# Second attention of a two-block layer: scores as three one-pass products, GpSimd beside the rotation of the queries

## What is computed

```python
def mla(c_q_raw, c_kv_raw, k_rope_raw, positions, q_norm, kv_norm, w_uq, w_ukv):
    q = (rmsnorm(c_q_raw, q_norm) @ w_uq).reshape(B, S, H, NOPE_DIM + ROPE_DIM)
    kv = (rmsnorm(c_kv_raw, kv_norm) @ w_ukv).reshape(B, S, H, NOPE_DIM + V_DIM)
    k_nope, v = kv[..., :NOPE_DIM], kv[..., NOPE_DIM:]
    cos, sin = rope_tables(positions, q.dtype)
    q_rope = apply_rope(q[..., NOPE_DIM:], cos[:, :, None, :], sin[:, :, None, :])
    k_rope = apply_rope(k_rope_raw, cos, sin)
    q_full = jnp.concatenate([q[..., :NOPE_DIM], q_rope], axis=-1)
    k_full = jnp.concatenate([k_nope, jnp.broadcast_to(k_rope[:, :, None, :], (B, S, H, ROPE_DIM))], axis=-1)
    return causal_block_attention(q_full, k_full, v)
...
def one_block(args):                       # in causal_block_attention
    s = jnp.einsum('bqhd,bkhd->bhqk', q_blk, k).astype(jnp.float32) * scale
    s = jnp.where(k_idx[None, :] <= q_idx[:, None], s, jnp.finfo(jnp.float32).min)
    pr = jax.nn.softmax(s, axis=-1)
    return jnp.einsum('bhqk,bkhd->bqhd', pr.astype(v.dtype), v)
```

## Time and profile before

| what | value |
|---|---|
| median of 3 runs | 899.24 us (898.68 to 899.51) |
| profiled execution | 898.62 us |
| its span | 896.9 us, mean granted clock of TensorE 0.999 of 2.4 GHz |
| busy: PE, DVE, ACT, POOL | 889.4, 398.5, 343.4, 497.5 us |
| first attention's steps | about 146 to 206 us |
| second attention's steps | about 387 to 450 us |

### The profile page before, as it was taken

One profiled execution on the slowest core, in us unless ns is written; L12 is line 12 of the kernel. 1 busy time (PEld: TensorE's weight loads), 2 busy tenths in 40 slices (PEclk: granted clock), 3 DMA queues, 4 the chain that ended last, 5 costly groups with the idle time before them and its releaser, 6 DMA issues.

```text
span 896.9 us, 12872 instructions
## 1 busy us (share of the span) xinstructions
PE 889.4 (99%) x4488; PEld 732.2 (82%) x4488; DVE 398.5 (44%) x690; ACT 343.4 (38%) x693; POOL 497.5 (55%) x515
## 2 busy tenths in 40 slices
PE   9999999999999999999999999999999999999998
PEld 7889887777779888876779888888888888888887
DVE  2753485677742743866667511111111112223672
ACT  4333403567715130566648532222222223233421
POOL 7988785321475877923336554444444445555453
PEclk9999999999999999999999999999999999999999
DMA  6342363212222422321013332233222323233213
GB/s 219 118 140 85 104 169 98 66 48 94 72 74 72 137 94 82 107 71 48 25 48 94 117 119 94 94 99 102 102 94 94 117 94 94 94 97 105 72 56 117
DMA packets 29467, 85.77 MB, mean 96 GB/s; under 512 B 5192, under 2 KB 8160, under 8 KB 29424
## 3 DMA queue, kind: packets, MB, share of 16 engines
q1 hardware_dynamic: 24528, 78.65, 26.7%
q10 hardware_dynamic: 4896, 6.53, 2.6%
HBM read 80.93 MB, written 2.10 MB: 93 GB/s over the span
## 4 chain that ended last, share of the span: by engine, by line
PE 96%; DVE 1%; ACT 1%; issue 1%; POOL 1%; ACTq 0%; POOLq 0%; DVEq 0%
PE bank L505 28%; PE bank L507 28%; PE bank L506 28%; PE bank L562 5%; PE bank L750 2%; PE bank L1085 2%; PE bank L849 1%; POOL w_lo L458 1%; PE bank L841 1%; PE bank L878 1%; ACT h L1486 0%; DVE negmax L2032 0%; PE bank L729 0%; DVE h L2039 0%; ACT PT L1330 0%
## 5 line engine op out<-in xcount | busy, mean ns | idle before, releaser
L458 POOL TENSOR_TENSOR w_lo<-raw,w_hi 128x256 fp32r<-128x256 f32 (+1 forms) x420 | 409.6, 1004 | 205.7 <-ACT w_hi L1330 199.8
L505 PE MATMUL bank<-aT_hi,w_hi 128*128 128x512 f32 (+1 forms) x584 | 225.8, 387 | 0.0
L507 PE MATMUL bank<-aT_hi,w_lo 128*128 128x512 f32 (+1 forms) x584 | 222.4, 381 | 0.0
L506 PE MATMUL bank<-aT_lo,w_hi 128*128 128x512 f32 (+1 forms) x584 | 222.2, 380 | 0.0
L505 PE MATMUL bank<-w_hi,aT_hi 128*128 128x512 f32 (+3 forms) x576 | 218.3, 379 | 0.5 <-POOL w_lo L458 0.4
L507 PE MATMUL bank<-w_hi,aT_lo 128*128 128x512 f32 (+3 forms) x576 | 213.0, 370 | 0.0
L506 PE MATMUL bank<-w_lo,aT_hi 128*128 128x512 f32 (+3 forms) x576 | 212.9, 370 | 0.0
L450 POOL TENSOR_SCALAR w_hi<-raw 128x1024 fp32r<-128x1024 f32 x70 | 77.3, 1105 | 173.7 <-PE bank L507 142.9
L1330 ACT ACTIVATE w_hi<-raw 128x1024 fp32r<-128x1024 f32 x70 | 74.1, 1060 | 231.4 <-PE bank L507 218.5
L507 PEld LDWEIGHTS bank<-aT_hi,w_lo 128*128 128x128 f32 x584 | 109.8, 188 | 20.9
L505 PEld LDWEIGHTS bank<-aT_hi,w_hi 128*128 128x128 f32 x584 | 110.2, 189 | 19.9 <-issue 0.2
(11 more groups left out here) (228 smaller groups left out, 887.6 us busy)
## 6 DMA issues: line engine op xcount, KB each, us to landing
raw<-in_weights SPq DMA_DIRECT2D x141, 512.0 KB, 3.3
x<-in_x ACTq DMA_DIRECT2D x4, 512.0 KB, 5.3
y_out<-x SPq DMA_DIRECT2D x7, 256.0 KB, 4.1
x<-in_x SPq DMA_DIRECT2D x3, 512.0 KB, 8.0
g_post<-in_gains ACTq DMA_DIRECT2D x3, 512.0 KB, 3.4
k_twice<-k_twice ACTq DMA_DIRECT2D x2, 512.0 KB, 5.7
x<-in_x SPq DMA_DIRECT2D x2, 256.0 KB, 3.9
raw<-in_weights SPq DMA_DIRECT2D x2, 256.0 KB, 4.2
```

The costliest lines, as they stand in the source:

```text
L458: lo = nc.gpsimd.tensor_tensor(w_lo[:, s, at], raw[:, r, at], w_hi[:, s, at].bitcast(F32), ALU.subtract)
L505: mm(out, st_hi, mv_hi, start=start, stop=False)
L506: mm(out, st_hi, mv_lo, start=False, stop=False)
L507: return mm(out, st_lo, mv_hi, start=False, stop=stop)
```

## The change

1. The scores of the second attention become three one-pass products: `q2_high` by `k2_high`, `q2_low` by `k2_high`, `q2_high` by `k2_low`. The key's and the query's high parts are written by ACT where it wrote `k2T` and `q2T`; DVE makes the low parts of both from the same banks and now frees these banks. The rotary rows of the keys' low part are made once and spread to the heads by two DMAs of ACT. The low parts of queries lie in `aT_hi` and `aT_lo`, those of keys in the arena and in the place of `g_post`.
2. DVE rotates query rows 0 and 2; POOL rotates rows 1 and 3, between the splits of chunk `uv` and chunk `out2c` 0. TensorE also waits for POOL's.
3. DVE's order ahead of the attention changes: `conv_lo` 2 and 3 go ahead of the rotations, the root's operations (`roots`) between the low parts of heads 2 and 3, and the low parts of heads 5 to 7 into steps 0 to 2 of the attention. On ACT the root's two operations go ahead of the copies of the queries.
4. In both attentions, at the end of a pair of heads, `beside` goes ahead of `values`.
5. The loads of `pe_raw` and `g_post` move to steps 24 and 32 of the second attention on ACT.

```diff
+            splits(0, CH["out2c"], False, parts=4)
+            pool.wait_ge(sines, 2)
+            rotate_q(1)
+            pool.wait_ge(pool_roped, 1)
+            rotate_q(3)
+            splits(CH["out2c"], SHARED, False, parts=4)
...
+                own(nc.gpsimd.tensor_tensor(by_cos, qr, cn, ALU.mult))
+                own(nc.gpsimd.tensor_tensor(by_sin, qr, sn, ALU.mult))
+                own(nc.gpsimd.tensor_tensor(qr[:, :, 0, :], by_cos[:, :, 0, :], by_sin[:, :, 1, :], ALU.subtract))
+                nc.gpsimd.tensor_tensor(qr[:, :, 1, :], by_cos[:, :, 1, :], by_sin[:, :, 0, :], ALU.add)\
+                    .then_inc(pool_roped, 1)
...
-                    if done >= 0 and done % (2 * T) == 2 * T - 1:
+                    pair_done = done >= 0 and done % (2 * T) == 2 * T - 1
+                    if pair_done:
+                        if m < steps:
+                            beside(m)
                         values(done // T - 1)
...
+            pe.wait_ge(pool_roped, 2)
             turn_heads("q2T", MLA_H, QK2, lambda t, i: q2[:, t, i * QK2:(i + 1) * QK2], roped, 2)
...
             def mla_score(out, i, qb, kw):
-                mm(out, q2T[0:QK2, i, qb * P:(qb + 1) * P], k2T[0:QK2, i, 0:kw], start=True, stop=False)
+                at = slice(qb * P, (qb + 1) * P)
+                if qb == 0:
+                    pe.wait_ge(q2_hi, i + 1)
+                    pe.wait_ge(q2_lo, i + 1)
+                mm(out, q2_high[0:QK2, i, at], k2_high[0:QK2, i, 0:kw], start=True, stop=False)
+                mm(out, q2_low(i)[0:QK2, at], k2_high[0:QK2, i, 0:kw], start=False, stop=False)
+                mm(out, q2_high[0:QK2, i, at], k2_low(i)[0:QK2, 0:kw], start=False, stop=False)
...
             softmax_attention(FOX_H * T, MLA_H, mla_score, v2, out2c_piece,
-                              first=lambda m: pe.wait_ge(drained["act"], tiles["q2T", 2][3][1]),
+                              first=lambda m: pe.wait_ge(drained["dve"], tiles["q2T", 2][3][1]),
...
+            act_.dma_start(k2_low_first[HD:QK2, :, :].bitcast(F32), rope_low.broadcast_to([ROPE, MLA_H - 2, S]))\
+                .then_inc(k2_rope_in, 16)
+            act_.dma_start(k2_low_last[HD:QK2, 1:2, :].bitcast(F32), rope_low).then_inc(k2_rope_in, 16)
...
+            for i in range(MLA_H):
+                full(act_, ("q2T", i))
+                copy(q2_high[0:QK2, i, :], tbank(("q2T", i))[0:QK2, :]).then_inc(q2_hi, 1)
...
+                if m == (MLA_H - 2) * T:
+                    act_.dma_start(pe_raw, pt_d).then_inc(pt_in, 16)
+                if m == MLA_H * T:
+                    act_.dma_start(g_post[:, :], gains_d[3, :, :]).then_inc(g_post_in, 16)
...
-            for t in range(T):
+            conv_lo(2)
+            conv_lo(3)
+            for t in (0, 2):
...
+            def q2_low_part(i):
+                dve.wait_ge(q2_hi, i + 1)
+                V.tensor_tensor(q2_low(i)[0:QK2, :], tbank(("q2T", i))[0:QK2, :],
+                                q2_high[0:QK2, i, :].bitcast(F32), ALU.subtract).then_inc(q2_lo, 1)
+                dve.wait_ge(q2_lo, i + 1)
+                order[0] += 1
+                assert tiles["q2T", i][3] == ("dve", order[0])
+                V.sem_inc(drained["dve"], 1)
...
+            for i in range(3):
+                q2_low_part(i)
+            roots(slice(60, 64))
             V.tensor_tensor(stat[:, 3, 60:64], stat[:, 3, 60:64], stat[:, 3, 4:8], ALU.mult).then_inc(group_rsqrt, 1)
+            for i in range(3, 5):
+                q2_low_part(i)
```

More of the change, by code:

```diff
@@ L478, in splits, with own, rotate_q @@
                     split(c, c % SLOTS, shared, skipped=skipped, own=own, parts=parts)
-            splits(0, SHARED, False, parts=4)
+            turns = [0]
+            def own(ins):
+                turns[0] += 1
+                ins.then_inc(pool_step, 1)
+                pool.wait_ge(pool_step, turns[0])
+            def rotate_q(t):
+                pool.wait_ge(drained["act"], tiles["uq", t, 1][3][1])
+                qr = q2[:, t, :].rearrange("p (h c) -> p h c", c=QK2)[:, :, HD:]\
+                    .rearrange("p h (a b) -> p h a b", b=HALF)
+                sn, cn = (cs[:, j, t, :].unsqueeze(1).unsqueeze(1).broadcast_to([P, MLA_H, 2, HALF]) for j in (0, 1))
+                by_cos, by_sin = (view(PTf, 512 + 2 * j * MLA_H * HALF, MLA_H, 2, HALF) for j in (0, 1))
+                own(nc.gpsimd.tensor_tensor(by_cos, qr, cn, ALU.mult))
[9 more added lines that the diff above has]
+            splits(CH["out2c"], SHARED, False, parts=4)
             splits(SHARED, CH["ffn"] + SLOTS, True, parts=4)
@@ L765, in softmax_attention @@
                     if m < steps:
-                        beside(m)
+                        if not pair_done:
+                            beside(m)
                     elif tail and m < steps + LAG and not (tail_first and m == steps):
@@ L1399, in qk_rows @@
                     nc.scalar.sem_inc(drained["act"], 1)
-            def heads_out(name, n, width, dst, scale=None):
-                for i in range(n):
-                    full(act_, (name, i))
-                    drain((name, i), copy(dst[0:width, i, :], tbank((name, i))[0:width, :],
-                                          1.0 if scale is None else scale))
             def heads_hi(name, dst, scale, made):
@@ L1416, in _ @@
             qk_rows("fq", 0)
-            act_.dma_start(g_post[:, :], gains_d[3, :, :]).then_inc(g_post_in, 16)
             act_.dma_start(g_col2[:, :], gains_d[1, 0, :].rearrange("(k p) -> p k", p=P),
@@ L1637, in _ @@
                     full(act_, ("krT", 0))
-                    own(copy(k2T[HD:QK2, 0, :], tbank(("krT", 0))[0:ROPE, :]))
-                    order[0] += 1
-                    assert tiles["krT", 0][3] == ("act", order[0])
-                    nc.scalar.sem_inc(drained["act"], 1)
-                    own(copy(k2T[HD:QK2, 1:, :], k2T[HD:QK2, 0:1, :].broadcast_to([ROPE, MLA_H - 1, S])))
+                    copy(k2_high[HD:QK2, 0, :], tbank(("krT", 0))[0:ROPE, :]).then_inc(k2_rope_hi, 1)
+                    act_.wait_ge(k2_rope_hi, 1)
+                    copy(k2_high[HD:QK2, 1:, :], k2_high[HD:QK2, 0:1, :].bitcast(F32)
+                         .broadcast_to([ROPE, MLA_H - 1, S])).then_inc(k2_rope_hi, 1)
             split_hi(aT_hi[:, 7, :], y[:, 3, :], col("gc", 3))
@@ L1648, in _ @@
                                              QK2 ** -0.5))
+            act_.wait_ge(k2_rope_lo, 1)
+            act_.wait_ge(mix_lo, 6 * T + KD + 9)
+            rope_low = k2_low_last[HD:QK2, 0:1, :].bitcast(F32)
+            act_.dma_start(k2_low_first[HD:QK2, :, :].bitcast(F32), rope_low.broadcast_to([ROPE, MLA_H - 2, S]))\
+                .then_inc(k2_rope_in, 16)
+            act_.dma_start(k2_low_last[HD:QK2, 1:2, :].bitcast(F32), rope_low).then_inc(k2_rope_in, 16)
             for i in range(4):
                 full(act_, ("uk", i))
-                own(copy(k2T[0:HD, 2 * i, :], tbank(("uk", i))[0:HD, :]))
-                drain(("uk", i), copy(k2T[0:HD, 2 * i + 1, :], tbank(("uk", i))[HD:P, :]))
+                copy(k2_high[0:HD, 2 * i, :], tbank(("uk", i))[0:HD, :]).then_inc(k2_hi, 1)
+                copy(k2_high[0:HD, 2 * i + 1, :], tbank(("uk", i))[HD:P, :]).then_inc(k2_hi, 1)
             for t in range(T):
@@ L2240, in _ @@
             V.sem_inc(roped, 1)
+            for i in range(4):
+                for n, r in enumerate((slice(0, HD), slice(HD, P))):
+                    dve.wait_ge(k2_hi, 2 * i + n + 1)
+                    V.tensor_tensor(k2_low(2 * i + n)[0:HD, :], tbank(("uk", i))[r, :],
+                                    k2_high[0:HD, 2 * i + n, :].bitcast(F32), ALU.subtract).then_inc(k2_lo, 1)
+                dve.wait_ge(k2_lo, 2 * i + 2)
+                order[0] += 1
+                assert tiles["uk", i][3] == ("dve", order[0])
+                V.sem_inc(drained["dve"], 1)
             full(dve, ("ssc", 0))
```

45 lines of the change are left out of this document (33 added, 12 removed).

## The result

| | median | runs | profiled execution | its span | mean granted clock |
|---|---|---|---|---|---|
| before | 899.31 us (898.68 to 899.91) | 11 | 898.62 us | 896.9 us | 0.999 |
| after | 902.16 us (899.77 to 903.21) | 11 | 902.63 us | 900.8 us | 0.996 |

The ratio is 1.0029 (95% interval 1.0020 to 1.0037): slower by about 0.3%, 2.3 us over the forecast and 0.2 us over the upper end of its range. (The forecast started from a median of 899.24 us for before; 1.0029 times that is 901.8 us, just inside the range.)

What follows compares the result with a forecast made beforehand. The prediction took TensorE, busy 99% of the span, to bound the kernel. Its terms -2.0 - 1.1 + 0 + 3.4 + 0.4 gave +0.7 us, so a median of 899.9 us, range 897.0 to 902.0.

Steps and rivals of the forecast that it cites:

- scores: Second attention: three one-pass products replace one full-precision product per score, saving 2.0 us over 8 heads (bounds -1.5 and -2.4).
- piece, first attention: Three 512-column products moved ahead of a pair's values cover waits in three pairs: -1.1 us (bounds -0.6 and -1.3).
- piece, second attention: The same move of three products ahead of the values in the second attention: 0 us (bounds -0.3 and +0.2).
- transposes to the first piece: Start of second attention: TensorE waits for DVE's low parts and the root's operations, first piece 3.4 us later.
- waits behind it: After the second attention's start, low parts 4 to 7 stand between DVE's first maxima: +0.4 us (bounds 0 and +1.2).
- sum without the clock: All forecast terms over both attentions added together: +0.7 us; the forecast had no clock term.
- DVE late: Rival: ahead of the second attention, ACT's root waits for DVE's mean, high parts 1.4 us later: 901.5 us; chance 0.12.
- scores without gain: Rival: in the second attention, short one-pass products do not hide each other's weights, scores save nothing: 901.9 us; chance 0.06.
- POOL slow on the rotations: Rival: POOL's query rotations take 2.4 us an operation on short runs, transposes start 6.3 us late: 906.2 us; chance 0.07.
- Clean start: Rival: second attention's start costs only +1.2 us, scores and piece give their upper bounds: 896.7 us; chance 0.18.
- likeliest case, no change: Whole kernel: median between 897.4 and 901.0 us, not told from no change; chance 0.60.
- cases for slower: Whole kernel over 901.0 us: DVE late (split), POOL slow on the rotations, scores without gain; slower had chance 0.23.

Runs made afterwards that it cites:

- e6_full_score: e5_root_late_act with each score of the second attention one full-precision product of the high parts, low-part products left out: 899.36 us.
- e4_piece_only: The kernel before with only the piece put ahead of the values at the end of a pair, in both attentions: 898.35 us, ratio 0.9988.
- e1_awake: The changed kernel with 18 unused transposes on TensorE between the second attention's first mask and the first piece: 900.16 us, ratio 1.0010.
- e5_root_late_act: e2_root_late with ACT's two root operations also moved, behind its copies of the queries: 898.28 us, ratio 0.9991.
- e2_root_late: The changed kernel with DVE's four tiny root operations moved behind low parts 3 to 7, into step 3 of the second attention: 898.17 us, ratio 0.9990.
- e3_pool_pause: The changed kernel with POOL waiting, ahead of its fourth out2c chunk, until the group's root is made: 900.25 us, ratio 1.0007.
- e8_before_hole: The kernel before with one added wait of TensorE for the group's root, ahead of the second attention's first piece: 902.38 us, ratio 1.0038.
- e10_low4_late: e5_root_late_act with the piece first in the first attention alone and head 4's low part behind the first maxima: 898.80 us, ratio 0.9996.
- e7_dve_rotates: The changed kernel with all four query rotations on DVE and none on POOL: 906.48 us, ratio 1.0081.

## Where the prediction was right and where it was wrong, step by step

| term | forecast | measured | from |
|---|---|---|---|
| scores | -2.0 | -1.4 | e6_full_score: 0.48 + 0.46 + 0.46 + 0 |
| piece, first attention | -1.1 | -0.94 | after, table above |
| piece, second attention | 0 | +0.2 | e4_piece_only: 3 x 0.07 |
| transposes to the first piece | +3.4 | +3.26 | 3.74 before, 7.00 after |
| waits behind it | +0.4 | +0.1 | e1_awake against e4_piece_only, below |
| sum without the clock | +0.7 | +1.2 | e1_awake: +1.25 between the medians |
| the clock | none | +1.6 to +2.3 | after against e1_awake |

In the medians that is 1.25 + 1.6 = 2.85 us, what after lies over its before, against the +0.7 of the forecast: 0.5 of the miss is in the terms, the rest is the clock.

- **The waits were read rightly.** The first score late by 0.9 us (0.75 was forecast), a hole of 2 to 3 us ended by the fourth low part, tiny DVE operations held by POOL (1.17 for two, against 1.18 in the earlier trace rows), 0.30 and 0.70 us for the scores of 128 and 512 columns (0.36 and 0.69 in after; the later 128-column ones take 0.29), values 0.33 behind the piece with no wait on ACT: each is in the rows of after.
- **The step that failed** is the sum itself. It priced a hole of 2 to 3 us at its own length, and every product behind it at the durations of rows taken at the clock's upper level. In the trace of before the granted clock is 1.00 in every stretch up to 890 us, so no row of it showed a hole in the middle of dense work; I should have bounded that cost, as the other unseen ones. In its place after shows 6.8 us at the lower level, which cost 1.6 to 2.3 us beside the 2.0 us idle: the hole costs about twice. That the time still lies within 0.2 us of the range is luck: its upper end stood for two rivals (DVE late, scores without gain) that did not happen.
- **Scores**, a size: -1.4 for -2.0. A head gave 0.23 us in the middle of the stage (0.27 was forecast), less at the start, where part of it goes into a longer wait for the probabilities, and nothing for the last head, behind which TensorE has no scores left and its transposes wait for the probabilities. I multiplied by 8 heads where the end of the stage is bound otherwise.
- **The waits behind the start**: transposes to the first values is 24.40 us in e1_awake and 21.54 in e4_piece_only; less 3.26 for the start and with 0.48 for the scores, 0.1 is left. That the late first piece gave DVE the time for low parts 4 to 7 is my reading of it, not a separate test. Where the start is repaired (e5_root_late_act), the waits come: mask to piece 0.26, and 0.40 on the probabilities.
- **Rivals.** DVE late for ACT: no. The mean was made at 382.39 and ACT's root began at 383.30, behind its own copy, so the margin was 0.9 us and not 0.2. DVE's two rotations took 5.3 us (369.00 to 374.27) where I had 6.6 from rows beside POOL. POOL slow on the rotations: no; they ended at 375.2:

```profile
369.71 0.77 POOL L508 TENSOR_TENSOR PT<-arena,cs 128x256 f32<-128x256 f32 x1 [1.18 <-ACT arena L1385]
370.56 0.73 POOL L509 TENSOR_TENSOR PT<-arena,cs 128x256 f32<-128x256 f32 x1
371.37 0.46 POOL L510 TENSOR_TENSOR arena<-PT 128x128 f32<-128x128 f32 x1
371.91 0.52 POOL L511 TENSOR_TENSOR arena<-PT 128x128 f32<-128x128 f32 x1
```

  Runs of 16 elements cost what contiguous ones do here (0.46 to 0.80 us an operation). The price that the Trainium skill, GPSIMD Engine Reference, section "7. Performance pitfalls for Q7 kernels", puts on each small read command, about 102 cycles, does not show in these rows. Scores without gain: no. Clean start: only with the root moved (e2_root_late).
- **The chances.** The likeliest case, no change, was not what came; slower had 0.23. None of my cases for slower was the cause.

What stays open: what decides from run to run whether the clock falls, and for how long. By the mean clock of each run, with a hole of 0.98 us behind a wait of 0.76 it fell in 6 runs of 10 (e3_pool_pause), with one of 2.12 us alone in 3 of 5 (e8_before_hole), in after in 9 of 11, and with 1.14 us alone in none of 11 (e10_low4_late).

## What to carry to other kernels

A wait of TensorE in the middle of dense work may have to be priced twice: for its length, and for the products behind it at the lower clock (1.3 to 2.6 us in the runs here in which it fell); a change that opens one of a microsecond or two should be judged over many runs, by the mean clock of each. Four tiny operations on the wrong side of a release decided this change: ahead of the low part that frees a bank they stood on the path, beside a GpSimd that held them to nearly three times their time, and in the fourth step of the attention nobody waited for them (POOL was idle by then too, and the chain took 0.66 us in e2_root_late). When an instruction gets shorter by so much, count only the stretches in which TensorE isn't waiting for someone else, and look at the last one, where the pipeline runs dry.

## What the runs showed of the hardware

- The granted clock of an otherwise busy TensorE fell to its lower level around idle times of 0.76 and 0.74 us close together (6 of 10 runs), 1.90 us (3 of 5) and 0.75 and 2.00 us (9 of 11), and not with 0.76 us (0 of 11) or 1.14 us (0 of 11) by themselves. For the first two kernels the idle times are from profiled executions in which the clock stayed up. In the two profiled executions that have the fall (after, e7_dve_rotates) it began inside the hole and lasted 6.8 us. 18 small transposes in the hole kept the clock up in all 11 runs. At the lower level a 512-column one-pass product takes 0.43 us from start to start, at the upper 0.23.
- DVE operations of 4 elements a row with two inputs in SBUF: 0.15 to 0.22 us with POOL idle, 0.25 to 0.6 beside its splits. One with a single input in SBUF: 0.17 and 0.67. The low parts, with one input in PSUM, took 0.69 us in both.
